# A mixer's projection matmuls with the high and low activation parts side by side: 512 and 256 columns in place of three times 256

## The reference, cut to what matters

```
pc = hc @ w_in[l][:, :COL_Q]          # context: two gates and the values
kcf, gcf, kcb, gcb, vc = _hgrn_inputs(pc, lb)
s_f = _final_state(kcf, vc, gcf); s_b = ...

px = hx @ w_in[l]                     # latent tokens: all columns
kxf, gxf, kxb, gxb, vx = _hgrn_inputs(px, lb)
o_x, _, _ = _bidir_hgrn(_query(px), kxf, gxf, kxb, gxb, vx, s_f, s_b)
mix_x = concat([_hgrn_readout(o_x, px[..., COL_G:COL_HY], ...),
                _hyena(px[..., COL_HY:], ...)])
x = x + mx[5] * (mix_x @ w_out[l])
```

## Time and profile before

| | |
|---|---|
| median of 3 runs | 2997.76 us (2997.66 to 2998.6) |
| span of the profiled execution | 2996.3 us (the page gives no other time for it; the median of the runs is 1.46 us above) |
| PE busy | 2959.0 us, 99% of the span |
| DVE / ACT / POOL busy | 2027.5 / 1159.4 / 148.3 us |
| mixer (context units, pairs, Hyena, output projection) | about 1556 to 2250 us of the span |

### The profile page before, as it was taken

One profiled execution on the slowest core, in us unless ns is written; L12 is line 12 of the kernel. 1 busy time (PEld: TensorE's weight loads), 2 busy tenths in 40 slices (PEclk: granted clock), 3 DMA queues, 4 the chain that ended last, 5 costly groups with the idle time before them and its releaser, 6 DMA issues. The chain is left out here.

```text
span 2996.3 us, 42446 instructions
## 1 busy us (share of the span) xinstructions
PE 2959.0 (99%) x15850; PEld 2521.0 (84%) x15850; DVE 2027.5 (68%) x2558; ACT 1159.4 (39%) x1473; POOL 148.3 (5%) x182
## 2 busy tenths in 40 slices
PE   7999999999999999999999999999999999999998
PEld 3588888888888888888889999999997888888887
DVE  4698667676766677774476567778866666666667
ACT  5322222222122222222247777754445444444444
POOL 3000000000000000000000033340000000000000
PEclk9999999999999999999999999999999999999999
DMA  9865546354566758573335554455565666666664
GB/s 368 333 210 185 180 140 198 128 175 147 161 222 220 253 167 278 187 242 98 97 90 175 174 168 149 150 161 179 166 204 166 187 194 189 189 190 189 192 192 155
DMA packets 369832, 558.00 MB, mean 186 GB/s; under 512 B 17764, under 2 KB 259809, under 8 KB 368946
## 3 DMA queue, kind: packets, MB, share of 16 engines
q1 hardware_dynamic: 364256, 543.05, 57.7%
q0 software_dynamic: 2640, 8.52, 0.9%
q10 hardware_dynamic: 2818, 4.82, 0.4%
HBM read 550.02 MB, written 6.30 MB: 186 GB/s over the span
## 5 line engine op out<-in xcount | busy, mean ns | idle before, releaser
L442 DVE TENSOR_TENSOR w_lo<-raw,w_hi 128x1024 fp32r<-128x1024 f32 x736 | 911.8, 1240 | 696.1 <-ACT w_hi L435 693.9
L435 ACT ACTIVATE w_hi<-raw 128x1024 fp32r<-128x1024 f32 x736 | 777.9, 1059 | 1478.3 <-PE bank L454 1095.0
L711 DVE SCALAR_TENSOR_TENSOR states<-ada_raw,silu_c,states 128x1024 f32<-128x1024 f32 x300 | 375.5, 1281 | 2.3
L452 PE MATMUL bank<-h_hi_early,w_hi 128*128 128x512 f32 x768 | 300.7, 392 | 2.1 <-issue 2.1
L454 PE MATMUL bank<-h_hi_early,w_lo 128*128 128x512 f32 x768 | 298.9, 389 | 0.0
L453 PE MATMUL bank<-h_lo_early,w_hi 128*128 128x512 f32 x768 | 298.8, 389 | 0.0
L458 PE MATMUL bank<-w_hi,h 128*128 128x512 f32 x736 | 287.7, 391 | 1.9 <-DVE h L559 1.3
L460 PE MATMUL bank<-w_lo,h 128*128 128x512 f32 x736 | 286.5, 389 | 0.0
L459 PE MATMUL bank<-w_hi,h 128*128 128x512 f32 x736 | 286.3, 389 | 0.0
L452 PE MATMUL bank<-h_hi_late,w_hi 128*128 128x512 f32 x704 | 274.0, 389 | 0.0
L454 PE MATMUL bank<-h_hi_late,w_lo 128*128 128x512 f32 x704 | 273.9, 389 | 0.0
(11 more groups left out here) (345 smaller groups left out, 4978.7 us busy)
## 6 DMA issues: line engine op xcount, KB each, us to landing
raw<-in_ffn_w_dram SPq DMA_DIRECT2D x528, 512.0 KB, 4.3
ada_raw<-in_ada_w_dram SPq DMA_DIRECT2D x252, 512.0 KB, 4.7
raw<-in_w_in_dram SPq DMA_DIRECT2D x176, 512.0 KB, 3.7
raw<-in_w_out_dram SPq DMA_DIRECT2D x32, 512.0 KB, 4.3
ada_ahead<-in_ada_w_dram SPq DMA_DIRECT2D x20, 512.0 KB, 17.6
raw<-in_ada_w_dram SPq DMA_DIRECT2D x8, 512.0 KB, 18.4
ada_more<-in_ada_w_dram SPq DMA_DIRECT2D x8, 512.0 KB, 6.9
spec<-spec_spill POOLq DMA_DIRECT2D x8, 512.0 KB, 3.9
```

The lines of the kernel that those rows point to most:

```text
L435: nc.scalar.activation(w_hi[un.slot(j)][:], raw[un.slot(j)][:], ACT.Copy).then_inc(hi_done, 1)
L442: nc.vector.tensor_tensor(w_lo[un.slot(j)][:], raw[un.slot(j)][:], w_hi[un.slot(j)][:].bitcast(F32), ALU.subtract).then_inc(lo_done, 1)
L452: nc.tensor.matmul(o, w_hi[slot][:, c0:c0 + P], hi, start=start, stop=False, skip_group_check=True)
L711: nc.vector.scalar_tensor_tensor(out=total, in0=src, scalar=silu_c[:, m, t:t + 1], in1=total, op0=ALU.mult, op1=ALU.add).then_inc(done, 1)
```

## The change

The two parts of the activations lie in one tile (`hx`, `hc`: part, block, token). One matmul of 512 columns multiplies the high weights with both parts at once, into a whole PSUM bank: high×low and high×high side by side (for the latent tokens the low part stands first). A second one of 256 columns adds low×high to the first half. So a block has two matmuls, not three, and each half b of the output channels needs a bank of its own: a projection part now takes a pair of banks, 0 and 1 or 2 and 3, in turn. The value units and the output projection stay as they were.

The two halves of a bank must still be added. DVE does it with a reduction over an innermost axis of two, from two PSUM banks (128 x 1024 read) into a tile in SBUF (128 x 512): `join`, once per part, 8 times for the context, 16 for the pairs and 12 for Hyena, 36 in all. It stands at the head of DVE's step t = 4, 8, 12, 20 (that is j = 0 of the next pair) of a pair, and at every fourth step of the Hyena stage, ahead of the weight tile's low part. PE waits for the join of two parts before. ACT and DVE read the joined tile (`c_whole`, `x_whole`, one buffer each; `u_even`, `u_odd`), so ACT's sigmoids wait for DVE; they are moved from j = 3 and 7 to j = 4 and 8, behind the older pair's exponentials of that step, the query from j = 11 to 12, the values from 15 to 16, the output gate from 19 to 20.

```diff
+        def paired_unit(pe, un, j, kg, base, both, hi, each=None):
+
+            pe.wait_ge(lo_done, un.number(j) + 1)
+            for k in range(4):
+                kb = 4 * kg + k
...
+                for b in range(2):
+                    c0 = k * 256 + b * P
+                    nc.tensor.matmul(bank[base + b], w_hi[un.slot(j)][:, c0:c0 + P], both(kb), start=(kb == 0), stop=False,
+                                     skip_group_check=True)
+                    last = nc.tensor.matmul(bank[base + b][:, 0:256], w_lo[un.slot(j)][:, c0:c0 + P], hi(kb), start=False,
+                                            stop=(kb == KB - 1), skip_group_check=True)
+            last.then_inc(w_used, 1)
+
+        def join(out, base):
+
+            return nc.vector.reduce_sum(out, banks[:, base:base + 2, :].rearrange("p a (s n) -> p a n s", s=2), mybir.AxisListType.X)
...
+        def hg_base(it, part):
+            return 2 * ((5 * it + part) % 2)
...
+                if j in (8, 12, 16):
+                    pe.wait_ge(joined, HG_JOINED + 4 * it + (j // 4 - 1))
...
-                    col_unit(pe, MX, 20 * it + j, j % 4, [bank[j // 4][:, 0:256], bank[j // 4][:, 256:512]],
-                             lambda k: hx_hi[:, k, :], lambda k: hx_lo[:, k, :], True)
+                    paired_unit(pe, MX, 20 * it + j, j % 4, hg_base(it, j // 4), lambda k: hx[:, :, k, :], lambda k: hx_hi[:, k, :])
...
-            def gates(s, d, b, k_ap, g_ap, value):
-
-                ac.wait_ge(w_used, value)
-                nc.scalar.activation(k_ap, bank[b][:], ACT.Sigmoid, scale=-1.0)
-                nc.scalar.activation(g_ap, bank[b][:], ACT.Sigmoid).then_inc(s["gate"], 1)
+            def gates(s, whole, count, k_ap, g_ap):
+
+                ac.wait_ge(joined, count)
+                nc.scalar.activation(k_ap, whole, ACT.Sigmoid, scale=-1.0)
+                nc.scalar.activation(g_ap, whole, ACT.Sigmoid).then_inc(s["gate"], 1)
...
             def hg_act(it, j):
...
-                if j in (3, 7):
-                    d = j // 4
-                    gates(xs, d, d, flat(xk[it % 2][:, d]), flat(xa[it % 2][:, d]), used(MX, 20 * it + j))
-                if j in (4, 8):
-                    d = j // 4 - 1
-                    keys_logs(xs, it, d, flat(xk[it % 2][:, d]), flat(xa[it % 2][:, d]), hg_cols[:, it])
...
+                if j in (4, 8):
+                    d = j // 4 - 1
+                    gates(xs, flat(x_whole[:]), HG_JOINED + 4 * it + d + 1, flat(xk[it % 2][:, d]), flat(xa[it % 2][:, d]))
+                    keys_logs(xs, it, d, flat(xk[it % 2][:, d]), flat(xa[it % 2][:, d]), hg_cols[:, it])
...
+            def hg_joined(it, part):
+
+                ve.wait_ge(w_used, used(MX, 20 * it + 4 * part + 3))
+                base = hg_base(it, part)
+                if part == 0:
+                    ve.wait_ge(xs["v"], 3 * it)
+                elif part < 3:
+                    ve.wait_ge(xs["gate"], 2 * it + part)
+                else:
+                    ve.wait_ge(xs["v"], 3 * it + 1)
+                join(x_whole[:], base).then_inc(joined, 1)
...
             for t in range(T_END):
+                if 0 < t <= T_HY and t % 4 == 0 and t % 20 != 16:
+                    hg_joined((t - 1) // 20, (t - 1) % 20 // 4)
+                if T_HY < t <= T_OUT and t % 4 == 0:
+                    hy_joined((t - T_HY - 1) // 12, (t - T_HY - 1) % 12 // 4)
                 rest_unit(ve, MX, t + AHEAD)
```

More of the change, by code:

```diff
@@ L259, in build @@
         ctok = sb("ctok", [P, 3, 4, P], scope=con)
+        c_whole = [sb(f"c_whole{n}", [P, 2, CTX], scope=con) for n in range(2)]
         con.close()
@@ L324, in build @@
         f2.close()
-        bank = [life.enter_context(nc.psum_tensor(f"bank{n}", [P, 512], F32)) for n in range(8)]
+        banks = life.enter_context(nc.psum_tensor("bank", [P, 8, 512], F32))
+        bank = [banks[:, n, :] for n in range(8)]
         gate_dram = nc.dram_tensor("gate_row_spill", [KB, P], F32, kind="Internal").ap()
@@ L1602, in hg_read @@
                                            (vtok[:, other, :], cross[:, other, :]))[n]
-                            ins = nc.tensor.matmul(bank[OUT_BANK[it]][:, at * P:(at + 1) * P], left, right, start=(n == 0 and at == 0),
+                            ins = nc.tensor.matmul(bank[OUT_BANK][:, at * P:(at + 1) * P], left, right, start=(n == 0 and at == 0),
                                                    stop=(n == 3), skip_group_check=True)
@@ L2341, in ctx_keys, with ctx_joined @@
                 nc.vector.tensor_tensor(ckd[:, d], ck[:, d], cexp[:, d], ALU.mult).then_inc(cs["kd"], 1)
+            def ctx_joined(it, d):
+                ve.wait_ge(w_used, used(Units(U_CTX, it, 12), CTX_END[it][d]))
+                if it:
+                    ve.wait_ge(cs["gate"], 2 * it + d - 1)
+                join(c_whole[d][:], ctx_base(it, d)).then_inc(joined, 1)
             for it in range(PAIRS):
@@ L2347, in _ @@
                 for j in range(12):
+                    for d in range(2):
+                        if j == CTX_END[it][1 if it == 0 else d] + 1:
+                            ctx_joined(it, d)
                     rest_unit(ve, un, j + AHEAD)
@@ L2461, in hg_dve, with hy_joined @@
                     hg_norm(it)
+            def hy_joined(p, c):
+                n = 3 * p + c
+                ve.wait_ge(w_used, used(MX, T_HY + 12 * p + 4 * c + 3))
+                if n == 0:
+                    ve.wait_ge(xs["v"], 3 * PAIRS)
+                if n > 1:
+                    ve.wait_ge(ys["cb"], n - 1)
+                join(u_whole[n % 2][:], hy_base(p, c)).then_inc(joined, 1)
             def hy_edges(p, c):
```

144 lines of the change are left out of this document (86 added, 58 removed).

## The result

Median of the changed kernel 3005.31 us (3004.14 to 3009.61, 9 runs), of the kernel before 2997.69 us (2997.41 to 2998.64, 9 runs): ratio 1.0027, 95% interval [1.0018, 1.0036]. The change makes the kernel 7.6 us slower. The forecast was 2996 us, 2 us less than before. The measured time lies just inside the stated range (2983 to 3006), but it moved the other way, and "slower" had a chance of 0.20. The profiled execution took 3005.13 us.

The account below looks back on a forecast made before the run. PE, 99% busy, was taken to bound the kernel, with the DVE and ACT chain close behind. Of 15.7 us saved on PE some 13.6 go to the chain: -2.1 us, about 2996 us, range 2983 to 3006 us.

Parts of the forecast that it names:

- context: Context units: joins and moved sigmoids cost nothing, so the full PE saving of 32 units counts, -3.5 us.
- handover to pair 1: From pair 0's chain to pair 1: the chain, with slack left, gives a delay of 0.8 us.
- two full cycles: Pairs 1 and 2: the chain leads, each pair taking 72.0 us instead of 70, so 2 × 2.0 us.
- last pair: Pair 3's chain: joins at t = 80 and 88 in DVE's unbroken sequence add 0.4 + 1.2 us.
- Hyena and `w_out`: After the pairs: units 91 to 93 give -0.3 us, one join delays `yf` by 1.2, later units give -3.2.
- fits into the same 70 us with 1.2 us to spare: In the pairs, the DVE and ACT chain was taken to have 1.2 us of room per 70 us pair.
- The saving on PE: Paired matmuls in 1152 blocks: 0.0136 us saved each, 15.7 us in all, 0.109 us per unit.
- The rule that was weighed: Skill page's column-independent cost of about 2.5 ns a matmul, saving an estimated 2.9 us; the forecast used 13.6 ns instead.
- The join: DVE's reduction over pairs from two banks: 1.2 us each, between 0.69 and 1.93 us; 36 joins are 43 us.
- Pairs, first stretch: Where pair 0's chain meets pair 1's gates: high parts start 1.25 us later, then 2.5 us later after the second sigmoids.
- The clock: Rival: new PE waits at four to six places drop the clock, adding 7 to 10 us, 3005 us; chance 0.05.
- slower by the join: Rival: a join takes 1.9 us, not 1.2, adding 8 us over about 11 joins on the chain, 3004 us; chance 0.13.

Follow-up runs that it names:

- Run 11: Kernel before, with one of the three matmuls of each block left out in the pairs' 64 units that are not values: 2990.76 us, ratio 0.9977.
- run 3: Changed kernel with the inputs laid out so that a block's high and low part are one stretch of 512 columns: 3006.56 us, ratio 1.0026.
- run 5: Changed kernel with the low weights' matmul also 512 columns wide, so all matmuls of a block have one width: 3105.54 us, one run.
- run 4: Changed kernel with the four matmuls of one k reordered, both of 512 columns first, then both of 256: 3004.96 us, ratio 1.0022.
- run 9: Changed kernel with each join replaced by a copy of the first halves of its two banks, 512 elements: 3000.76 us, ratio 1.0008.
- run 1: Changed kernel with joins, banks and sigmoids kept, but each block again three matmuls of 256 columns: 3009.71 us, ratio 1.0038.
- run 2: Changed kernel without the joins of context and pairs; ACT reads the first halves of the two banks itself: 3001.69 us, ratio 1.0013.
- run 8: Changed kernel with paired matmuls and joins only in context and Hyena, the pairs as in the kernel before: 2998.78 us, ratio 1.0003.
- run 6: Changed kernel with a gate's sigmoids and logarithms ahead of the older pair's exponentials at j = 4 and 8, joins kept: 3005.70 us, ratio 1.0025.
- run 7: Run 2 with the pairs' sigmoids back ahead of the older exponentials at j = 3 and 7: 2997.13 us, ratio 0.9997.
- run 12: Changed kernel with a unit's 8 matmuls of 512 columns first and its 8 of 256 columns behind them: 3005.26 us, ratio 1.0023.

## Why the prediction was wrong, step by step

The sum, place by place, in us against the kernel before. The first two lines make up PE's lead at the first read-out, and the third is what the handover to pair 1's level 0 keys takes of it:

| | forecast | measured |
|---|---|---|
| context | -3.5 | -0.6 |
| pair 0, to its read-out (19 units in the forecast) | -2.1 | -1.1 |
| handover to pair 1 | +0.8 | +1.6 |
| two full cycles | +4.0 | +6.0 |
| last pair | +1.6 | +2.0 |
| Hyena and `w_out` | -2.9 | -1.2 |
| sum | -2.1 | +6.8 |

Of the 8.9 us between the sums, some 5.6 are PE's saving that was not there, or was waited off outside the pairs' chain (lines 1, 2 and 6), and some 3.2 are the chain in the pairs (lines 3 to 5).

**The chain: "fits into the same 70 us with 1.2 us to spare" failed.** The 1.21 us of DVE's idle time ahead of the level 0 keys are time in which PE reads out. I took them as spare room of the whole loop. Run 11 shows that the loop needs 69.8 us and more by itself, with PE 15.4 us faster; 0.2 to 0.3 us were spare. So the full cycle, forecast at 72.0 us, is 73.0, and the handover takes 1.6 us and not 0.8: the direction and the mechanism were right (joins in DVE's queue, second sigmoids held up by a join), and nothing was there to absorb a part of it. With that, 4.7 us of the forecast's lead are gone at pair 1's level 0 keys, which come 0.1 us before their old time and not 4.8; 3.9 of them PE never had.

**The saving on PE: 15.7 us, measured 8.9.** The blocks' 422.0 us include some 1.5 us lost to the lower clock at their start, the 414.3 after some 2.7 (below): 420.5 - 411.6 = 8.9 us, 7.7 ns a block in place of 13.6, and 0.062 us a unit in place of 0.109. The term that failed is the difference 3 × 0.1200 - (0.2264 + 0.1200): it takes each width's time from a row of its own kind, and side by side they take longer. ("So I add nothing for that", on the two stretches, was right by run 3.) Two paces occur, each constant in a unit, in PE's timeline of the changed kernel:

```profile
1559.12 0.40 PE L519 MATMUL bank<-hc,w_parts 128*128 128x512 f32 x1
...
1573.26 0.40 PE L519 MATMUL bank<-hc,w_parts 128*128 128x512 f32 x1
...
1975.29 0.40 PE L519 MATMUL bank<-hx,w_parts 128*128 128x512 f32 x1
...
1980.15 0.39 PE L519 MATMUL bank<-hx,w_parts 128*128 128x512 f32 x1
```

40 blocks in 14.14 us are 0.3535 each, 14 blocks in 4.86 us are 0.347: the forecast's 0.3464, but only in 57 of 144 units, and in 2 of the context's 32. Run 3 excludes the two stretches and run 5 a slower wide matmul as such; the order within a k has a part in it (run 4: no unit at 0.3535). Why a unit falls into one pace or the other is open. The rule that was weighed was 2.5 ns a matmul, an estimated 2.9 us in all (the Trainium skill, TensorE: Matmul & The Clock Gate, section "Wait — 56ns, not 53.3ns?"). The trace does not agree with it: 8.9 us are nearly as far from it as from my 15.7.

**The join: 1.2 us, right.** The groups of DVE in the changed kernel:

```profile
L527 DVE TENSOR_REDUCE x_whole<-bank 128x512 f32<-128x1024 f32 x16 | 19.4, 1214 | 0.6 <-PE bank L521 0.6
```

It takes 1.214 us, near the 1.240 us of the subtraction over 1024 elements. The copy of 512 elements out of the same two banks takes 0.68 us (run 9), near the 0.692 us of a reduction of 512. So in these rows the time goes with the elements read, and two banks cost nothing on top.

**The context: -3.5 us forecast, -0.6 measured.** "I cost the joins at nothing" failed, and with it the new place of the sigmoids, which I had put at nothing too. Nearly all of its units run at the slow pace (some 1.3 us saved on its blocks, without the clock), and at 1592.6 us PE waits 2.0 us for the low part of the next pair's first unit. ACT's timeline there:

```profile
1581.77 1.28 ACT L1909 ACT_TABLE_LOAD   x1 [1.07 <-DVE c_whole L527]
...
1590.16 1.04 ACT L443 ACTIVATE w_parts<-raw 128x1024 fp32r<-128x1024 f32 x1
```

ACT waits 1.07 us for the joins, does the sigmoids and logarithms of both gates, and only then the high part whose low part PE needs. I had seen that ACT waits for PE there, and not that a high part stands behind the gates. In runs 1, 2 and 3, whose mixer begins at the lower clock like the one before, ACT has no wait for a join there; it waits 1.42, 1.36 and 1.16 us for PE at the tile that the sigmoids now stand behind. So the sigmoids' new place alone can bring PE's wait of 0.8 to 0.9 us; no run moves them back here, so this is argued and not shown.

The 1.5 us at the lower clock with which the mixer of before begins don't occur in this execution, but that was no luck. The low part comes 36.6 us after the mixer's first matmul whether the clock was low at the start (runs 3 and 8) or not (the changed kernel, runs 4 and 6); PE's wait is 0.9 and 1.0 us in the first case and 2.0, 2.3 and 2.4 in the second. In run 3 the first latent unit starts 147.2 us after the first matmul, in the changed kernel 147.1.

**Pairs, first stretch: right in kind, 0.6 to 1 us short each.** Exponentials ended at 1855.5 (forecast 1854.9), high parts at 1861.05 (1860.3), second joined tile at 1870.4 (1869.6), high parts at 1874.7 (1873.7). Wrong in that account is the part of the order on ACT: I drew the delay from the sigmoids' new place behind the exponentials, but with joins it makes no difference (run 6); it costs 1.0 us a pair only without them (runs 2 and 7). What lengthens the pair is DVE's time in joins, about two of four on the chain (run 9).

**The last pair and Hyena.** The last pair's chain lost 2.0 us more where +1.6 was forecast, and Hyena with `w_out` gave back 1.2 us where 2.9 was. `yf` holds PE for 0.6 us, the fold for another 0.4; the 32 units at 0.062 us are 2.0 us and not 3.5.

**The clock: no term of the sum, a rival with 0.05.** Two of the four waits of 2 us and more were followed by a stretch at the lower level, 1.2 GHz (windows of the changed kernel: length, PE, PEld, DVE, ACT, POOL, granted clock, DMA share, GB/s):

```profile
1866.00:1868.00 2.00, 2.00 (x8) 1.71 (x8) 1.69 (x3) 1.98 (x3) 0.00 (x0) 0.50 0.68 190
...
1938.00:1940.00 2.00, 2.00 (x16) 1.83 (x15) 1.70 (x4) 2.00 (x4) 0.00 (x0) 1.00 0.72 238
...
2010.00:2012.00 2.00, 2.00 (x8) 1.71 (x8) 2.00 (x4) 0.84 (x1) 0.00 (x0) 0.51 0.28 63
```

A block takes 0.64 us there and not 0.35. Four blocks behind the wait of 2.66 us and five behind that of 2.35 lose 2.7 us, and eight scores at 1864.67 take 1.30 us to the next start, where 0.81 is the mean, 0.5 us more. The waits of 2.48 us ahead of 1938 and of 2.02 us had none behind them.

On PE's timeline these are 3.2 us, but they lengthened nothing: PE would have waited instead. The cycle with such a stretch is 73.01 us long, the next one without it 72.99. Run 3 has none behind its wait of 2.66 us, and there PE stands for another 1.20 us at the scores of the next pair's chain, which the changed kernel does not:

```profile
1908.99 1.16 PE L1626 MATMUL bank<-lq,lk 128*128 128x128 f32 x8 [1.20 <-DVE lk L2479]
```

At the last pair the read-out comes 63.95 us after the level 0 keys in the changed kernel, with a stretch at the lower level, and 63.98 us in run 1, with none. So this rival has no share in the result of this execution: in the pairs the chain sets the time, not PE's clock.

Together, on PE's timeline and against the forecast's -2.1: 8.9 us saved, 13.0 us of waits more, 1.7 us net at the lower clock (3.2 less the 1.5 at the start of before), and 1.0 us in small differences, +6.8. Waits and clock are one sum here: what the clock takes in the pairs, the waits would. The rival "slower by the join" named the outcome and almost the time (3004), but its reason didn't hold and its number is luck: a join costs 1.2 us and not 1.9. At 1.2 us it is enough, since the chain had no room and PE saved little.

## What to carry to other kernels

An engine's idle time ahead of one instruction is slack only against the work that it waits for; whether a loop over several engines has room is seen by asking what closes it, and can be measured by leaving out work of the engine that seems to lead (run 11): if the period stays, that engine's savings are worth nothing there. A loop can be at its limit on two sides at once: here PE shows 99%, and the chain over DVE and ACT, 68% and 39% busy, is just as long. And work added to a queue with 30% of free time costs its full length at the few places where that queue is on the chain; count how many of these places the new work has (here about two joins of four).

## What the runs showed of the hardware

- Matmuls of 512 and 256 columns in turn take 0.3465 or 0.3535 us for the two, at one pace through a unit of 8; two and two in turn 0.347 to 0.351 (run 4), eight and eight 0.349 (run 12). Each width by itself takes 0.2272 (run 5) and 0.1200 us. I had expected the sum of the two everywhere.
- A reduction over pairs out of two PSUM banks takes 1.21 us for 1024 elements read and 512 written, a copy of 512 out of two banks 0.68 us (run 9).
- PE's lower clock level did not follow the length of an idle stretch alone: it came after waits of 2.66, 2.35 and 1.87 us (run 9) and not after others of 2.66 (run 9), 2.48 and 2.30 us (run 2), and the same 2.64 us at the start of the mixer had it in some executions and not in others. Each time it cost PE some 1.5 to 1.7 us of work; in the pairs, where PE waits for the chain, that did not lengthen the cycle.
